# A two-block transformer kernel on one core: landing places for weight pieces in the mixing stage, and a new order of squares and gate products in the joining stage

## What is computed

```python
def chunk_gmlp(u, v, ln_g, ln_b, w_s, b_s):
    vn = layer_norm(v, ln_g, ln_b).reshape(B_, n, CHUNK, B_GROUPS, B_GROUP_DIM)
    s = jnp.einsum('gpq,bnqgc->bnpgc', w_s, vn) + jnp.transpose(b_s)[None, None, :, :, None]
    return u * s.reshape(B_, L, B_WIDTH)
...
    b = chunk_gmlp(gelu(u), gelu(vv), ln_g, ln_b, w_s, b_s)
    y = (jnp.concatenate([a, b], axis=-1) * jax.nn.silu(gate)) @ w_out
...
    x = x + gate_l * yl          # context rows: xc + gate_c * yc
    hl = rms_norm(x, norm_g[layer]) * (1.0 + scale_l) + shift_l
```

## Time and profile before

| what | us |
|---|---|
| median of 3 runs (4340.15 to 4352.18) | 4348.42 |
| the profiled execution, its own time | 4352.67 |
| its span in the trace | 4350.9 |
| PE busy in the span | 3569.0 (82%) |
| DVE busy | 1700.0 (39%) |
| ACT busy | 1109.2 (25%) |
| POOL busy | 1093.7 (25%) |
| mixing stage, first load issued to last work | 799.07 to 1016.7 |
| joining stage, first load issued to last work | 3547.11 to 3716.9 |

### The profile page before, as it was taken

One profiled execution on the slowest core, in us unless ns is written; L12 is line 12 of the kernel. 1 busy time (PEld: TensorE's weight loads), 2 busy tenths in 40 slices (PEclk: granted clock), 3 DMA queues, 4 the chain that ended last, 5 costly groups with the idle time before them and its releaser, 6 DMA issues. The chain is left out here.

```text
span 4350.9 us, 58360 instructions
## 1 busy us (share of the span) xinstructions
PE 3569.0 (82%) x23778; PEld 2730.5 (63%) x23778; DVE 1700.0 (39%) x2371; ACT 1109.2 (25%) x2069; POOL 1093.7 (25%) x775
## 2 busy tenths in 40 slices
PE   3599688498767999977999999887599958579991
PEld 0599544287654555556888888665588856556660
DVE  4401344363145666644255111354344446111113
ACT  0111122342231333332253111352232333011111
POOL 0000123230032444411243454101444412110002
PEclk7799788699887999998999999998899989589995
DMA  7222200442364221043233221226444345299965
GB/s 272 94 75 76 76 5 10 142 149 79 75 247 98 66 69 48 13 133 119 73 86 102 75 76 50 60 71 196 116 118 111 105 157 203 100 353 329 327 221 203
DMA packets 346451, 541.50 MB, mean 124 GB/s; under 512 B 60927, under 2 KB 230655, under 8 KB 343777
## 3 DMA queue, kind: packets, MB, share of 16 engines
q1 hardware_dynamic: 325470, 479.00, 35.1%
q10 hardware_dynamic: 13184, 33.56, 2.4%
q0 software_dynamic: 7568, 25.70, 1.6%
HBM read 398.48 MB, written 139.71 MB: 124 GB/s over the span
## 5 line engine op out<-in xcount | busy, mean ns | idle before, releaser
L2318 PE MATMUL mx_ps_p<-mx_wh,h 128*128 128x512 f32 x1280 | 397.4, 391 | 0.0
L455 PE MATMUL in_ps_p<-in_wh,h 128*128 128x352 f32 x1280 | 311.0, 325 | 11.5 <-DVE in_wl L468 11.5
L2318 PEld LDWEIGHTS mx_ps_p<-mx_wh,h 128*128 128x128 f32 x1280 | 242.0, 189 | 50.6
L1878 ACT ACTIVATE la_pt<-la_ps_s 128x1024 f32<-128x1024 f32 x160 | 164.0, 1025 | 399.9 <-PE la_ps_s L1840 399.9
L3776 PE MATMUL ex_ps_g<-ex_wgu,ex_xt 128*128 128x256 f32 x1024 | 234.4, 388 | 27.0 <-ACT ex_xt L3810 13.3
L1840 PE MATMUL la_ps_s<-la_q,la_k 104*128 104x512 f32 x960 | 254.2, 400 | 2.5 <-DVE la_q L1920 2.5
L1795 POOL TENSOR_TENSOR la_accp<-la_accp,la_pt 128x1024 f32<-128x1024 f32 x80 | 195.2, 2440 | 229.2 <-ACT la_pt L1878 229.2
L2318 PE MATMUL mx_ps_p<-mx_wl,h 128*128 128x512 f32 x640 | 250.4, 391 | 0.0
L2311 PE MATMUL mx_ps_p<-h,mx_wh 128*128 128x512 f32 x768 | 238.5, 392 | 0.0
L3776 PEld LDWEIGHTS ex_ps_g<-ex_wgu,ex_xt 128*128 128x128 f32 x1024 | 195.7, 194 | 60.6 <-DVE ex_xt L3827 19.2
L455 PEld LDWEIGHTS in_ps_p<-in_wh,h 128*128 128x128 f32 x1280 | 223.5, 188 | 11.9 <-DVE in_wl L468 11.9
(11 more groups left out here) (597 smaller groups left out, 7258.2 us busy)
## 6 DMA issues: line engine op xcount, KB each, us to landing
ex_wgu<-in_moe_w_gate_dram SPq DMA_DIRECT2D x32, 1024.0 KB
ex_wgu<-in_moe_w_up_dram SPq DMA_DIRECT2D x32, 1024.0 KB
ex_wd<-in_moe_w_down_dram SPq DMA_DIRECT2D x32, 1024.0 KB, 9.5
ada_w<-in_w_ada_dram SPq DMA_DIRECT2D x12, 2048.0 KB, 18.2
mx_w<-in_w_in_dram SPq DMA_DIRECT2D x16, 1024.0 KB, 5.4
mx_w<-in_w_in_dram SPq DMA_DIRECT2D x32, 512.0 KB, 4.7
dl_row<-rows SPq DMA_DIRECT2D x32, 512.0 KB, 4.7
yb<-ex_y SPq DMA_DIRECT2D x32, 512.0 KB, 6.3
```

The costliest lines, as they stand in the source:

```text
L455: mm = te.matmul(ps[n % NB][:, 0:cw], a, b, start=k == 0 and n_ == 0, stop=k == kt - 1 and n_ == 2)
L1878: act.activation(pt[t % NPT][:], ps[t % 2][:], ACT.Exp, scale=scale).then_inc(*act_s.did(flat(o)))
L2318: mm = te.matmul(ps[bank[n] // 2][:, bank[n] % 2, :], a, b, start=k == 0 and m == 0, stop=k == KT - 1 and m == 2)
```

## The change

Mixing stage: each of the 8 weight pieces gets its own landing place and semaphore. Two of them are the old weight buffers, the others are `ht`, `xr`, `ga_t` and `sh_t`, which are not needed yet at that time. The loads that need these places (`res(0)`, `res(1)`, the gate and shift rows) wait for the `wl` of the piece. `tile(2)` is issued before the scale rows, the residuals and the gate and shift rows. The context rows are fetched in steps 3 and 6 of SP's loop; `gs_0` moves behind `mb_1`, `gs_1` to step 5.

Joining stage: `mx` is split into `ma` (the 4 products into a) and `mx` (the 8 into f). ACT does `sa`, `sf` of tile t+3 as the last work of step t, no longer those of tile t+2 ahead of `hi`. DVE's step becomes xs, ea, ex, ma, hn, lo, mx, ad; POOL's pa, px, fb.

```diff
-            dve_order += ["gs_0", "cs_0"] + [f"wl_{n}" for n in range(NW // 2)]
+            dve_order += ["cs_0"] + [f"wl_{n}" for n in range(NW // 2)]
...
-            dve_order += [f"wl_{n}" for n in range(NW // 2, NW)] + ["gs_1"]
+            dve_order += [f"wl_{n}" for n in range(NW // 2, NW)]
+        if t == -1:
+            dve_order += ["gs_0"]
+        if t == 5:
+            dve_order += ["gs_1"]
...
+        w_in = [st.sem(f"w_in{n}") for n in range(NW)]
+        land = [wt[0][:], wt[1][:]] + [flat(b[:]) for b in (ht[0], ht[1], xr[0], xr[1], ga_t, sh_t)]
...
-                    if n >= 2:
-                        sp.wait_ge(*dve.at(f"wl_{n - 2}"))
-                    sp.dma_start(wt[n % 2][:], w.rearrange(...)...).then_inc(w_in[n % 2], 16)
+                    sp.dma_start(land[n], w.rearrange(...)...).then_inc(w_in[n], 16)
...
                 sp.dma_start(cst[:], row_of(ln_b)).then_inc(lb_in, 16)
-                weight(0)
-                weight(1)
-                sp.dma_start(lg[:], row_of(ln_g)).then_inc(lg_in, 16)
                 sp.dma_start(bs[:], b_s.rearrange("g p -> p g"), allow_slow_non_contiguous=True).then_inc(bs_in, 16)
                 local(0)
+                for n in range(NW // 2):
+                    weight(n)
+                sp.dma_start(lg[:], row_of(ln_g)).then_inc(lg_in, 16)
                 tile(1)
+                for n in range(NW // 2, NW):
+                    weight(n)
+                local(1)
+                tile(2)
                 sp.dma_start(sc_t[:], row_of(scale[0])).then_inc(sc_in, 16)
                 sp.dma_start(g_t[:], row_of(norm_g)).then_inc(sc_in, 16)
-                for n in range(2, NW):
-                    weight(n)
-                local(1)
+                for t in both:
+                    sp.wait_ge(*dve.at(f"wl_{4 + t}"))
+                    res(t)
+                sp.wait_ge(*dve.at("wl_6"))
                 sp.dma_start(ga_t[:], row_of(gate[0])).then_inc(ga_in, 16)
+                sp.wait_ge(*dve.at("wl_7"))
                 sp.dma_start(sh_t[:], row_of(shift[0])).then_inc(sh_in, 16)
-                for t in both:
-                    res(t)
-                sp.wait_ge(*dve.at(f"wl_{NW - 1}"))
-                sp.dma_start(line(wt[1]), row_of(scale[1])).then_inc(c_in, 16)
-                sp.dma_start(line(wt[0]), row_of(gate[1])).then_inc(cga_in, 16)
-                sp.wait_ge(*dve.at("gs_1"))
-                sp.dma_start(g_t[:], row_of(shift[1])).then_inc(csh_in, 16)
-                for t in range(-1, NT):
+                for t in range(NT):
...
+                    if t == 3:
+                        sp.wait_ge(*dve.at(f"wl_{NW - 1}"))
+                        sp.dma_start(line(wt[1]), row_of(scale[1])).then_inc(c_in, 16)
+                        sp.dma_start(line(wt[0]), row_of(gate[1])).then_inc(cga_in, 16)
+                    if t == 6:
+                        sp.wait_ge(*dve.at("gs_1"))
+                        sp.dma_start(g_t[:], row_of(shift[1])).then_inc(csh_in, 16)
...
-    act_order += [..., "wh_2", "wh_3", "sa_1", "sf_1"]
+    act_order += [..., "wh_2", "wh_3", "sa_1", "sf_1", "sa_2", "sf_2"]
...
-                         (act_order, (("sx", t - 1), ("sa", t + 2), ("sf", t + 2), ("hi", t + 1), ("ht", t - 2))),
-                         (dve_order, (("xs", t - 1), ("ex", t - 1), ("ea", t + 2), ("lo", t + 1), ("hn", t - 1), ("mx", t + 2), ("ad", t + 2))),
-                         (pool_order, (("px", t - 1), ("pa", t + 2), ("fb", t + 3)))):
+                         (act_order, (("sx", t - 1), ("hi", t + 1), ("ht", t - 2), ("sa", t + 3), ("sf", t + 3))),
+                         (dve_order, (("xs", t - 1), ("ea", t + 2), ("ex", t - 1), ("ma", t + 2), ("hn", t - 1), ("lo", t + 1), ("mx", t + 2), ("ad", t + 2))),
+                         (pool_order, (("pa", t + 2), ("px", t - 1), ("fb", t + 3)))):
...
-                    elif nm == "mx":
+                    elif nm == "ma":
                         ve.wait_ge(*pool.at(f"pa_{t}"))
                         ve.wait_ge(g2_in[s], 32 * (t // 2 + 1))
```

More of the change, by code:

```diff
@@ L948, in mix_out @@
             (st.sem(n) for n in ("ws_in", "lb_in", "lg_in", "bs_in", "sc_in", "ga_in", "sh_in", "c_in", "csh_in", "cga_in"))
-        w_in, x_in, a_in, r_in, x_st = ([st.sem(f"{n}{s}") for s in both] for n in ("w_in", "x_in", "a_in", "r_in", "x_st"))
+        w_in = [st.sem(f"w_in{n}") for n in range(NW)]
+        x_in, a_in, r_in, x_st = ([st.sem(f"{n}{s}") for s in both] for n in ("x_in", "a_in", "r_in", "x_st"))
         pe, act_s, dve, pool = (Order(st.sem(n), o) for n, o in (("pe", pe_order), ("act", act_order), ("dve", dve_order), ("pool", pool_order)))
         rows = lambda t: slice(t * P, (t + 1) * P)
+        flat = lambda t: t.rearrange("p (q n) -> p q n", q=QK)
+        land = [wt[0][:], wt[1][:]] + [flat(b[:]) for b in (ht[0], ht[1], xr[0], xr[1], ga_t, sh_t)]
         g3 = lambda t: t.rearrange("p (g n) -> p g n", g=G)
@@ L972, in weight @@
                     c, q = pieces[n]
-                    if n >= 2:
-                        sp.wait_ge(*dve.at(f"wl_{n - 2}"))
-                    sp.dma_start(wt[n % 2][:], w.rearrange("(k p) n -> p k n", p=P)[:, q * QK:(q + 1) * QK, c * BANK:(c + 1) * BANK]).then_inc(w_in[n % 2], 16)
+                    sp.dma_start(land[n], w.rearrange("(k p) n -> p k n", p=P)[:, q * QK:(q + 1) * QK, c * BANK:(c + 1) * BANK]).then_inc(w_in[n], 16)
                 def tile(t):
@@ L1004, in _ @@
                 sp.dma_start(cst[:], row_of(ln_b)).then_inc(lb_in, 16)
-                weight(0)
-                weight(1)
-                sp.dma_start(lg[:], row_of(ln_g)).then_inc(lg_in, 16)
                 sp.dma_start(bs[:], b_s.rearrange("g p -> p g"), allow_slow_non_contiguous=True).then_inc(bs_in, 16)
                 local(0)
+                for n in range(NW // 2):
+                    weight(n)
+                sp.dma_start(lg[:], row_of(ln_g)).then_inc(lg_in, 16)
                 tile(1)
+                for n in range(NW // 2, NW):
+                    weight(n)
+                local(1)
+                tile(2)
                 sp.dma_start(sc_t[:], row_of(scale[0])).then_inc(sc_in, 16)
                 sp.dma_start(g_t[:], row_of(norm_g)).then_inc(sc_in, 16)
-                for n in range(2, NW):
-                    weight(n)
-                local(1)
+                for t in both:
+                    sp.wait_ge(*dve.at(f"wl_{4 + t}"))
+                    res(t)
+                sp.wait_ge(*dve.at("wl_6"))
                 sp.dma_start(ga_t[:], row_of(gate[0])).then_inc(ga_in, 16)
+                sp.wait_ge(*dve.at("wl_7"))
                 sp.dma_start(sh_t[:], row_of(shift[0])).then_inc(sh_in, 16)
-                for t in both:
-                    res(t)
-                sp.wait_ge(*dve.at(f"wl_{NW - 1}"))
-                sp.dma_start(line(wt[1]), row_of(scale[1])).then_inc(c_in, 16)
-                sp.dma_start(line(wt[0]), row_of(gate[1])).then_inc(cga_in, 16)
-                sp.wait_ge(*dve.at("gs_1"))
-                sp.dma_start(g_t[:], row_of(shift[1])).then_inc(csh_in, 16)
-                for t in range(-1, NT):
-                    if 2 <= t + 3 < NT:
+                for t in range(NT):
+                    if t + 3 < NT:
                         tile(t + 3)
@@ L1109, in _ @@
                         c, q = pieces[t]
-                        act.wait_ge(w_in[s], 16 * (t // 2 + 1))
-                        op = act.activation(wh[c][:, q * QK:(q + 1) * QK, :], wt[s][:], ACT.Copy)
+                        act.wait_ge(w_in[t], 16)
+                        op = act.activation(wh[c][:, q * QK:(q + 1) * QK, :], land[t], ACT.Copy)
                     elif nm == "gv":
@@ L1144, in _ @@
                         ve.wait_ge(*act_s.at(f"wh_{t}"))
-                        op = ve.tensor_tensor(wl[c][:, q * QK:(q + 1) * QK, :], wt[s][:], wh[c][:, q * QK:(q + 1) * QK, :].bitcast(F32), ALU.subtract)
+                        op = ve.tensor_tensor(wl[c][:, q * QK:(q + 1) * QK, :], land[t], wh[c][:, q * QK:(q + 1) * QK, :].bitcast(F32), ALU.subtract)
                     elif nm == "gs":
@@ L3286, in join_out @@
     pe_order, act_order, dve_order, pool_order = ["T_0"], [], [], []
-    act_order += ["wh_0", "wh_1", "sa_0", "sf_0", "hi_0", "wh_2", "wh_3", "sa_1", "sf_1"]
-    dve_order += ["wl_0", "wl_1", "ea_0", "mx_0", "ad_0", "lo_0", "wl_2", "wl_3", "ea_1", "mx_1", "ad_1"]
+    act_order += ["wh_0", "wh_1", "sa_0", "sf_0", "hi_0", "wh_2", "wh_3", "sa_1", "sf_1", "sa_2", "sf_2"]
+    dve_order += ["wl_0", "wl_1", "ea_0", "ma_0", "mx_0", "ad_0", "lo_0", "wl_2", "wl_3", "ea_1", "ma_1", "mx_1", "ad_1"]
     pool_order += ["fb_0", "pa_0", "fb_1", "pa_1", "fb_2"]
@@ L3476, in _ @@
                             at = slice(h * GV, (h + 1) * GV)
-                            ve.scalar_tensor_tensor(a[s][:, at], a[s][:, at], ss[s][:, h:h + 1], ga[s][:, at], ALU.mult, ALU.mult)
```

(3 more changed lines are left out.)

## The result

The changed kernel takes 4309.6 us (median of 4, 4307.9 to 4310.8) against 4350.3 (4 runs), ratio 0.9905, 95% interval 0.9886 to 0.9924: the medians are 40.7 us apart, and the interval of the ratio reaches from 33 to 50 us. The forecast was 41.0 us, to 4307.5. The profiled execution took 4307.9, span 4306.1.

A forecast was written before the change was run, and what follows sets the result against it. No engine was taken to limit the whole span; waits bounded the mixing stage's start and a DVE-ACT loop the joining stage. -26.5 - 16 + 1.5 = -41.0 from 4352.7 gives 4311.7, less 4.2 for the runs' median 4307.5 us; range 4298 to 4325.

The forecast's parts named there:

- Mixing stage, start: Mixing stage up to G0_0: earlier wl_0, mb_0 and tile(2) bring G0_0 from 864.98 to 838.5, gain 26.5 us, bounds 20 to 28.
- rival of a start bound by its loads: Mixing stage start: loads bind, not waits; pieces 7 us late, gain 19 us, time 4315; chance 0.10.
- reason given for wl_0: Mixing stage, DVE: with gs_0 and its 5.30 us row wait gone, wl_0 follows wh_0 at 815.1 instead of 819.46.
- Joining stage: Joining stage: moving ACT's squares removes DVE's waits of 3.79 and 0.67 us; gain 16 us, possible ends 0 and 18.
- I take 13.0: Joining stage: a tile's period of 13.0 us, between TensorE's 12.8 and a two-tile chain's 13.05.
- G0_2 stays: Joining stage, first tiles: bound by their loads and ad_1 as before, so G0_2 stays at 3616.99.
- The chain's 2.1 for a collision with fb: Joining stage, two-tile chain: ma takes 2.1 us more where POOL's fb overlaps it; left in the 26.1 us for two tiles.
- rival "ACT stuck at sa": Joining stage: ACT waits at sa_{t+3} for a and holds sx_t, so nothing is gained; time 4323.4; chance 0.17.
- limits that the prediction set as signs of being wrong: Joining stage: ACT idle before sa for more than some 5 us and xs to xs staying over 15.
- The argument against the rival: Joining stage: in the new order f and b are issued some 7 us before a, no longer 1 us.
- the forecast's 13.05 beside 12.8: Joining stage, per tile: 13.05 us from the two-tile chain through a's landing, 12.8 from TensorE's work.
- Clearing: Stage boundaries: six more semaphores move the clearing to latent attention and add one after the experts' second pass; +1.5 us, between 0 and 2.

The follow-up runs named there:

- gs0_back: Changed kernel with gs_0 again ahead of cs_0 and wl_0, its two rows loaded ahead of the weight pieces; G0_0 39.2 us after the stage's first load, mixing stage 191.0.
- a_behind: Changed kernel with the joining stage's load of a issued behind both gate loads; joining stage 159.8 us against 152.8, 14.1 us a tile.
- two_places: Changed kernel with the mixing stage's weight pieces landing in two buffers in turn again; G0_0 49.4 us after the first load, mixing stage 201.2, joining stage 155.9.
- both_starts: Changed kernel with z_0 and mb_0 earlier in mixing, tile 1's squares and products earlier in joining; 4299.2 us, ratio 0.9886 to the kernel before.
- a_three: Changed kernel with three buffers for a in the joining stage, so its load waits for T_{t-3}; joining stage 153.8 us against 152.8.

## Why the prediction was right, step by step

- **Mixing stage, start: 26.5 forecast, 27.0 measured (G0_0 from 65.9 to 38.9), with two errors that largely cancel.** wl_3 ends 21.6 us after the first load, not 20.7 (the first two wl took 3.66 and not 2.35, one of them beside POOL's ma_0, which took 2.24). z_0 to mb_0 took 6.44 of 6.45. tile(2) had landed 5.0 after its issue, 6.5 forecast; a context row issued just ahead of it before, and not now, is the likely reason. gv_2 to G0_0 is 5.75 of 5.74.
- **The loads follow.** ACT waited for no piece. bs and local(0) ahead of them cost SP 3.13 us, less than the 4.82 in the earlier trace rows. So the rival of a start bound by its loads fell. gs0_back put 1 MB more in front of the pieces, and even that moved G0_0 by only 0.4 us.
- **The reason given for wl_0** was half right: moving gs_0 in DVE's list was not needed, only an earlier load of its row (gs0_back).
- **Mixing stage, the rest: 0 forecast, 0 measured.** Behind G0_0 the stage takes 152.2 us, 152.0 before.
- **Joining stage: 16 forecast, 19.0 measured.** The mechanism held, the term was mis-sized: "I take 13.0" a tile, and it is TensorE's 12.70, 1.5 us over five tiles. "G0_2 stays" was 1.5 us off; H_0 had waited 1.40 for hn_0 before and doesn't now. The chain's 2.1 for a collision with fb was too much on average: in the new order fb mostly meets mx, 3.2 us there in place of 2.18. It is right for a tile whose squares are late: in a_behind and in two_places ma then met fb and took 3.9 us.
- **The rival "ACT stuck at sa"** did not happen, but it is near: an identical joining stage took 152.8 to 155.9 us, in two_places with one tile of 16.6 in which ACT waited 5.3 for a (both over the limits that the prediction set as signs of being wrong, in that one tile), and a_behind shows 7 us for a landing 1.6 later. The argument against the rival was too strong: f is issued 3.4 to 4.4 us before a in the changed kernel, not 7, and 1.1 to 3.2 before. That the stage has so little room is what the forecast's 13.05 beside 12.8 said.
- **Clearing: +1.5 forecast, 1.4 to 1.5 measured**, at the places named.
- **The sum: -41.0 forecast, medians 40.7 apart.** That they agree to 0.3 us is luck: by the stages the change is worth 26.9 + 19.0 - 1.4 = 44.5 us, 3.5 more than forecast, most of it in the joining stage, and the whole runs tell it no better than 33 to 50. The two profiled executions differ by -1.4 us ahead of the mixing stage, -26.9 in it, +3.4 between the stages, -19.0 in the joining stage and -0.9 behind it, which makes the 44.8 of their spans. The +3.4 is not the change's: this stretch between the two stages takes 2528.7 to 2536.6 us over all these executions.

## What to carry to other kernels

Follow the first product of a stage back to the load that it waits for, and ask what stands in front of that load in its queue, not only how fast the weights come: here the order was worth more than the buffers. When an engine's list closes a loop with another engine's, move the work that belongs to a later tile behind the work of this one, and try each list by itself: one of the two reorderings here was the whole gain that shows, and the other, alone, a loss. Then look at what the moved work waits for; here it is a load with under two microseconds to spare (a landing 1.6 later cost 7 us in a_behind).

## What the runs showed of the hardware

- Ahead of any change, the mixing stage's start lies between 788.1 and 811.7 us after the span's start in the executions profiled, while the stage of the first projection begins within 2.2 us (162.3 to 164.5). In the window from 560 to 640 us (window attention), the granted clock was 0.95 in the earliest of them, both_starts, and 0.75 in gs0_back, the latest:
```profile
560.00:640.00 80.00, 65.90 (x346) 35.44 (x346) 34.58 (x46) 19.72 (x29) 27.18 (x19) 0.95 0.03 7
```
```profile
560.00:640.00 80.00, 69.36 (x291) 34.67 (x287) 27.94 (x37) 18.58 (x26) 23.40 (x15) 0.75 0.02 4
```
  In these 80 us TensorE ran 346 instructions in the one and 291 in the other, of a stage that is the same in both. This spread is as large as one part of the change, and it is why the stage lengths were used. What decides the clock there stays open.
- The joining stage moved 333 GB/s at DMA share 0.92 over two tiles, and a's landing over the stage was 6.1 us in the median, no slower than the 6.4 before, with 252 GB/s in a tile. That f and b, issued earlier, were out of its way is the likely reason; a_three, where a goes out right behind b, has 7.6 and fits it, but it wasn't tried by itself.
- Where DVE's products meet POOL's addition fb, they lose about what is left of fb when they begin: 2.1 of 2.3 us in the earlier trace rows; in the changed kernel 2.2 of 2.4 (mx at 3627.01 took 4.35 us in place of 2.18) and 1.0 of 1.2 (mx at 3613.67, 3.19). fb, beginning 0.2 us into a product of 1.28 (hn at 3611.33), took 3.3 us in place of 2.4. So the loss depends on which of the two begins first, and when; this is read from rows, no run was made for it.
- With the gaps gone the granted clock over the five tiles from G0_2 to G0_7 is 1.00, 0.92 before.
